# Experts' weights brought in twelve parts of 256 KB, released one by one by TensorE's products, instead of three transfers of 1 MB at once

## What is computed

```python
def expert_choice_ffn(h, router, e_gate, e_up, e_down):
    cap = EC_FACTOR * t // N_EXPERTS           # 128 sample tokens, 16 prompt tokens
    aff = jax.nn.softmax(jnp.einsum('btd,de->bte', h, router).astype(jnp.float32), axis=-1)
    gate, idx = lax.top_k(jnp.swapaxes(aff, 1, 2), cap)
    xe = h[bidx, idx]
    hid = jax.nn.silu(jnp.einsum('becd,edf->becf', xe, e_gate)) * jnp.einsum('becd,edf->becf', xe, e_up)
    ye = jnp.einsum('becf,efd->becd', hid, e_down) * gate[..., None].astype(h.dtype)
    return jnp.zeros_like(h).at[bidx, idx].add(ye)
```

## Time and profile before

| | |
|---|---|
| median of 3 runs | 3662.31 us (3658.36 to 3662.4) |
| the profiled execution's own time | 3664.57 us |
| its span, first to last instruction | 3662.8 us |
| PE busy | 3345.7 us (91%) |
| DVE busy | 2133.3 us (58%) |
| DMA, mean over the span | 183 GB/s |
| mean granted TensorE clock | 0.98 |

### The profile page before, as it was taken

One profiled execution on the slowest core, in us unless ns is written; L12 is line 12 of the kernel. 1 busy time (PEld: TensorE's weight loads), 2 busy tenths in 40 slices (PEclk: granted clock), 3 DMA queues, 4 the chain that ended last, 5 costly groups with the idle time before them and its releaser, 6 DMA issues.

```text
span 3662.8 us, 154096 instructions
## 1 busy us (share of the span) xinstructions
PE 3345.7 (91%) x72354; PEld 2883.5 (79%) x72354; DVE 2133.3 (58%) x3890; ACT 764.4 (21%) x1815; POOL 384.6 (10%) x536
## 2 busy tenths in 40 slices
PE   7989898998999986699999999999999999999998
PEld 3575767666555543599999999999999999999997
DVE  3567566665344445556566566565656565665655
ACT  3434344443344432000000000000000000000002
POOL 0142415243211000000000000000001000000001
PEclk9999999999999987799999999999999999999999
DMA  8200000000311131878778777777778777877775
GB/s 348 70 5 9 18 9 17 10 14 4 101 32 26 42 110 58 304 258 282 264 276 276 267 280 264 275 271 267 267 268 281 263 270 271 284 269 266 270 269 191
DMA packets 500361, 670.98 MB, mean 183 GB/s; under 512 B 31598, under 2 KB 438406, under 8 KB 496654
## 3 DMA queue, kind: packets, MB, share of 16 engines
q1 hardware_dynamic: 494030, 641.74, 49.8%
q0 software_dynamic: 5520, 19.34, 2.5%
q10 hardware_dynamic: 176, 0.05, 0.0%
HBM read 631.68 MB, written 28.30 MB: 180 GB/s over the span
## 4 chain that ended last, share of the span: by engine, by line
PE 56%; issue 3%; DVE 0%; DMA 0%; ACT 0%; DVEq 0%; POOLq 0%
PE banks L2508 34%; PE banks L2533 20%; PE banks L2449 2%; DMA e_xe<-scratch_h2d,idx 0%; DVE e_wgu L2812 0%; DVE e_wgu L2881 0%; DVE e_xe L2870 0%; DVE e_wsum L2720 0%; DVE e_wsum L2725 0%; DVE e_wgu L2715 0%; ACT e_xp L2648 0%; ACT e_xT L2648 0%; DVE e_wsum L2710 0%; DVE e_ye L2783 0%; DVE e_xpT L2729 0%
## 5 line engine op out<-in xcount | busy, mean ns | idle before, releaser
L2533 PE MATMUL banks<-e_hid,e_wd 128*64 128x144 f32 x11264 | 1273.1, 287 | 21.2 <-issue 18.1
L2533 PEld LDWEIGHTS banks<-e_hid,e_wd 128*64 128x64 f32 x11264 | 768.5, 137 | 32.9 <-issue 32.5
L2508 PE MATMUL banks<-e_xsum,e_wgu 128*64 128x72 f32 x11264 | 524.6, 227 | 32.2 <-issue 31.7
L2508 PE MATMUL banks<-e_xsum,e_wsum 128*64 128x72 f32 x11264 | 525.9, 227 | 25.9 <-issue 23.8
L2508 PEld LDWEIGHTS banks<-e_xsum,e_wgu 128*64 128x64 f32 x11264 | 499.4, 138 | 36.4 <-issue 35.8
L2508 PEld LDWEIGHTS banks<-e_xsum,e_wsum 128*64 128x64 f32 x11264 | 501.3, 137 | 31.3 <-issue 29.0
L2508 PE MATMUL banks<-e_xT,e_wgu 128*64 128x72 f32 x11264 | 515.5, 227 | 10.7 <-issue 10.5
L2743 DVE TENSOR_TENSOR e_gu<-e_first,banks 128x288 f32<-128x288 f32 x176 | 80.0, 455 | 762.3 <-ACT e_first L2629 565.3
L2508 PEld LDWEIGHTS banks<-e_xT,e_wgu 128*64 128x64 f32 x11264 | 496.6, 137 | 13.6 <-issue 13.6
L2629 ACT ACTIVATE e_first<-banks 128x144 f32<-128x144 f32 x176 | 51.1, 290 | 1518.7 <-PE banks L2508 1518.7
L2508 PE MATMUL banks<-e_xT,e_wsum 128*64 128x72 f32 x5632 | 263.0, 227 | 22.7 <-issue 22.3
(11 more groups left out here) (401 smaller groups left out, 4750.1 us busy)
## 6 DMA issues: line engine op xcount, KB each, us to landing
e_wgu<-in_e_gate SPq DMA_DIRECT2D x176, 1024.0 KB, 5.4
e_wgu<-in_e_up SPq DMA_DIRECT2D x176, 1024.0 KB, 8.7
e_wd<-in_e_down SPq DMA_DIRECT2D x176, 1024.0 KB
h_wmod<-in_w_mod SPq DMA_DIRECT2D x24, 1024.0 KB, 15.3
wblk<-in_w_in SPq DMA_DIRECT2D x22, 512.0 KB, 21.7
h_x<-in_x_sample SPq DMA_DIRECT2D x8, 512.0 KB, 6.9
wo<-in_w_out SPq DMA_DIRECT2D x2, 2048.0 KB, 12.0
scratch_ffn<-hT_x SPq DMA_DIRECT2D x8, 512.0 KB, 5.1
```

The costliest lines, as they stand in the source:

```text
L2508: last = nc.tensor.matmul(bank[4 + 2 * (n % 2) + g][c, q * HT:(q + 1) * HT], a[:, k, c], b[:, k, :], start=(k == 0), stop=(k == HALF - 1))
L2533: last = nc.tensor.matmul(bank[k // PER_BANK][c, at:at + TOK], wd[n % WD][:, b, k * P + h * CH:k * P + (h + 1) * CH], hid[n % 2][:, b, :], ...
```

## The change

Each piece of 1 MB is cut into four parts of 256 KB (`PARTS` = 4): gate and up into pairs of the eight k blocks, in the same rows of 1 KB, down into its two row blocks by two halves of 512 columns, so in rows of 2 KB. A new semaphore `pace` is incremented by TensorE at the end of each product but the last of a duo, 13 times per duo. Before part i of gate and up of duo n (i = 0 to 7) SP waits until duo n - 3 has done i + 1 products; before part i of down (i = 0 to 3) until it has done 9 + i. The wait for `used` stands between the two. For the first four duos there is no waiting for `pace`. The totals that PE and DVE wait for are raised, since each part adds 16.

```diff
+    PARTS = 4
+    GATE_UP_IN, DOWN_IN = 2 * PARTS * 16, PARTS * 16
...
-        used = sem("duo_used")
+        used, pace = sem("duo_used"), sem("products_done")
...
-                    if n >= WG:
-                        sp.wait_ge(gu_ps, n - WG + 1)
-                    sp.dma_start(wgu[n % WG][:, 0, :, :], gv[:, e, :, f]).then_inc(g_in[n % WG], 16)
-                    sp.dma_start(wgu[n % WG][:, 1, :, :], uv[:, e, :, f]).then_inc(g_in[n % WG], 16)
+                    for i in range(2 * PARTS):
+                        g, k = i // PARTS, slice(i % PARTS * 2, i % PARTS * 2 + 2)
+                        if n >= WG:
+                            sp.wait_ge(pace, (STEPS - 1) * (n - WG + 1) + i + 1)
+                        sp.dma_start(wgu[n % WG][:, g, k, :], (gv, uv)[g][:, e, k, f]).then_inc(g_in[n % WG], 16)
                     if n >= WD:
                         sp.wait_ge(used, n - WD + 1)
-                    sp.dma_start(wd[n % WD][:, :, :], dv[:, e, j * DUO:(j + 1) * DUO, :]).then_inc(d_in[n % WD], 16)
+                    for i in range(PARTS):
+                        b, d = j * DUO + i // 2, slice(i % 2 * 512, i % 2 * 512 + 512)
+                        if n >= WG:
+                            sp.wait_ge(pace, (STEPS - 1) * (n - WG + 1) + 2 * PARTS + i + 1)
+                        sp.dma_start(wd[n % WD][:, i // 2, d], dv[:, e, b, d]).then_inc(d_in[n % WD], 16)
...
                         last = product(n, 0, q)
                         if mats(n) == 2:
+                            last.then_inc(pace, 1)
                             done = downs(done, STEPS * n + 2 * q)
                             last = product(n, 1, q)
...
-                        if q == QS - 1:
-                            last.then_inc(gu_ps, 1)
+                        last.then_inc(gu_ps if q == QS - 1 else pace, 1)
                         done = downs(done, STEPS * n + 2 * q + 1)
```

More of the change, by code:

```diff
@@ L2525, in down @@
                     if r == 0:
-                        pe.wait_ge(d_in[n % WD], 16 * (n // WD + 1))
+                        pe.wait_ge(d_in[n % WD], DOWN_IN * (n // WD + 1))
                         pe.wait_ge(hid_ok, n + 1)
@@ L2588, in _ @@
                         pe.wait_ge(xs_ok, e + 1)
-                    pe.wait_ge(g_in[n % WG], 32 * (n // WG + 1))
+                    pe.wait_ge(g_in[n % WG], GATE_UP_IN * (n // WG + 1))
                     if n >= 2:
@@ L2708, in sums_first @@
                     a11, a12, a21, a22 = weight_blocks(n)
-                    dve.wait_ge(g_in[n % WG], 32 * (n // WG + 1))
+                    dve.wait_ge(g_in[n % WG], GATE_UP_IN * (n // WG + 1))
                     V.tensor_tensor(weight_sum(n, 0), a11, a21, ALU.subtract).then_inc(ws_ok, 1)
```

## The result

The changed kernel takes 3555.72 us (median of 4 runs, 3544.2 to 3559.09), against 3660.34 for the kernel before, also in 4 runs: ratio 0.971, 95% interval 0.9686 to 0.9734, so 105 us less. The profiled execution took 3554.39, its span 3552.7.

What follows compares the result with a forecast made beforehand. The prediction took PE as the bound, stopped by instruction packets late behind unbroken weight traffic. From the profiled 3664.6 us, 140 for stops and 2 for the clock gave 3522.6, or 3520 from the median; range 3506 to 3579.

Steps and rivals of the forecast that it cites:

- Half of it stays: Rival: instruction fetches may suffer from any full traffic, so half of the 142 us gain is lost, 3591 us; chance 0.10.
- The bound and its cause: Expert stage's steady part: PE the only bound, idle 136.9 us in 172 stops because instruction packets come late behind weight bursts.
- 152 us for all stops together: PE's 172 stops in the steady part: 136.9 us idle plus some 0.09 us each beside it.
- What of it stays: Stop time left in the steady part after the change: 12 us, ends 0 and 46, making the term -140 us.
- Clock, 2 us: PE's granted clock, 0.50 for 3.4 us after the 2.73 us stop: -2 us, ends 0 and -4.
- Signals 0: The added signal on each product, 13 per duo: costs 0, ends 0 and 23 us.
- SP 0: SP issuing twelve parts and waiting thirteen times per duo: 4.4 of 12 us, so it costs 0.
- Parts later, 0: Every weight part issued later: 18 us of cover against 5.4 us from issue to landing of 1 MB, so 0.
- Rows of 2 KB, 0: Down's transfers in rows of 2 KB for 4 KB: 0.69 us per part, still under 0.75, so 0.
- The queue never runs dry: Rival: parts join into a burst of 12 products, 400 fetches stop instead of 172, +201 us, 3863; chance 0.07.
- Each part pays a whole start: Rival: each part pays 2.6 us fixed start in series, 39 us per duo against 12, 8.4 ms; chance 0.02.

Runs made afterwards that it cites:

- the floor: Kernel before with weights brought only for the first four duos (down: six), later duos computing with what the tiles hold: 3516.91 us, ratio 0.9602.
- half of the bytes: Changed kernel with each part moving half of its 256 KB from the fifth duo on (down: seventh): 3513.5 us, ratio 0.9616.
- At 24: Changed kernel with 24 parts of 128 KB, two per product, down's cut into quarters of the partitions: 3939.57 us, ratio 1.0783.
- the table of four: Three transfers of 1 MB or twelve parts of 256 KB, at once or paced by products: 3660 and 3630 us at once, 3588 and 3556 paced.

## Why the prediction was right, and which term was off

The time, 3555.72, lies in the forecast's own range (3506 to 3579) and the mechanism was the forecast's: the stops fell from 172 to 58 and PE remained the bound. The size was less well met. 105 us were gained where 142 were forecast, and 3555.72 lies midway between the forecast's 3520 and the 3591 of the rival "Half of it stays". The median duo went from 12.0 us to 11.6 (from one first copy of ScalarE to the next), not to 11.3.

- *The bound and its cause.* Right. "issue" of PEld was a lack of instructions made by the weights' traffic: without later weights 5 stops are left, and 171 of the 172 ended just behind a packet of instructions.
- *152 us for all stops together.* Near: the floor is 143 us below before in one job's medians, and half of the bytes brings 138.
- *What of it stays: taken as 12 us, ends 0 and 46.* This is the step that was off. It measured 41.5 us of idle and 58 x 0.09 = 5 us beside it, 47 us, just past the far end. Two readings in it failed. I took the stretch from 3 to 5 us after the issue as "full traffic" with 1.0% idle. But a packet feeds PE for 5.3 us, so a stop there most likely answers to a fetch of the time before the burst (worked out, not shown singly); in the changed kernel, with traffic always, idle is 42.4 of 2014 us, 2.1%, as in the first three us of before. And I let the new ring run dry between parts, at 378 GB/s and 0.69 us per part; the share of 0.90 in place of the 0.8 that I wrote suggests that it seldom does. Half of the bytes, where it does, brought the floor.
- *Clock, 2 us.* Fits what is left of the account, not shown singly.
- *Signals 0.* Right, 0.9991. *SP 0.* Right at twelve parts: one issue per product. At 24 it would have been wrong: SP's issues, 0.47 us apart, then fill 11.4 us of a duo. *Parts later, 0.* Right: DVE waited for them twice, 5.9 us.
- *Rows of 2 KB, 0.* They cost little: a packet of 2 KB takes 84 ns (median) and one of 4 KB 159. But the term looked at the rows alone: with parts of the same size in rows of 4 KB over half of the partitions the gain is nil. The cutting of down by columns in place of partitions is a part of what makes the change work.
- *Rivals.* "Half of it stays" lay on the right side of the error: fetches do suffer from any nearly full traffic. "The queue never runs dry" named the right danger and the wrong price: the DMA share is 0.90 all the time, and stops fell all the same. I take it that a fetch finds less ahead of it when the transfers are short and few of them stand in the ring; the table of four agrees, but no trace shows the order in the ring. "Each part pays a whole start" is refused at 256 KB; at 128 KB the bringing of weights did become the bound, but a duo took 13.8 us and not 24 starts of 2.6. The fit that the prediction took from the Trainium skill (DMA: Bandwidth & Descriptors, the table of fixed and variable cost) is one of transfers issued from GpSimd, and these come from SP.
- *The Trainium skill's rule* (Runtime: NRT & Kernel Launch, Instruction fetch mechanics) that the fetch is hidden doesn't hold beside this stage's weights: 143 us hang on it. Without them 5 stops are left, and the trace nearly agrees.

## What to carry to other kernels

Where a matmul engine is the bound and its idle time has "issue" as the only releaser, look at the instruction queue in the DMA list: instructions per packet, how long one lasts, and how long weight traffic runs without a break. Bring the bytes in transfers that each cover all partitions, released by the consumer's own progress; a transfer per product of 0.75 us was best here, and smaller ones gained nothing. Measure the floor once with the traffic left out, and once with half of it, before tuning the order.

## What the runs showed of the hardware that I had not expected

- PE stopped for want of instructions 172 times, 0.8 us each, while the instruction queue took 1.0% of the DMA engines' time.
- Equal bytes, sizes and moments, but down cut by partitions into rows of 4 KB: DMA share 0.96 against 0.90, and 97 us. The median packet of 4 KB took 248 ns over 64 partitions, 159 over 128.
- At equal bytes and moments six transfers of 512 KB left 79.2 us of idle, twelve of 256 KB 46.1, and 16 with half of gate and up at 128 KB 47.4. Three of 1 MB, begun four products apart, left 74.9, in as many stops as the six (109). Why six are no better than three, and how much of the rest is the transfer's size and how much down's rows of 4 KB, stays open.
- Spreading the same transfers over two issuing engines left more stops, 70 against 58.
- 171 of 172 stops ended 0.9 to 1.7 us after the end of an instruction packet, so such a stop can be told from others in the packet records.
